# Second block: the selected and local scores of two heads issued in pairs, the compressed mask added once per bank

## The reference, cut to what matters

```
s_c = einsum(qq, kc);  p_c = masked_softmax(s_c, cmp_end <= t)      # compressed: 15 keys
...
s_s = einsum(qq, k_g); m_s = tok <= t                                # selected blocks
p_s = masked_softmax(s_s, m_s)
...
s_w = einsum(qq, kwb)                                                # local window of 512
p_w = masked_softmax(s_w, m_w)
return gg[0] * o_c + gg[1] * o_s + gg[2] * o_w
```

## Time and profile before

| | |
|---|---|
| median of 3 runs | 969.4 us (962.84 to 970.59) |
| profiled execution | 968.41 us |
| its span in the trace | 966.7 us |
| TensorE / VectorE / ScalarE / GpSimd busy | 93% / 71% / 53% / 33% |
| mean granted TensorE clock | 0.952 |

### The profile page before, as it was taken

How to read it: one execution, slowest core, us unless ns; L and a number is a source line. 1 busy time by engine, 2 the same in 40 slices (tenths; PEclk the granted TensorE clock), 3 DMA queues, 4 the chain that set the end, 5 groups by cost and what they waited for, 6 DMA issues and landing times.

```text
span 966.7 us, 16928 instructions
## 1 busy us (share of the span) xinstructions
PE 897.8 (93%) x6718; PEld 855.5 (88%) x6718; DVE 683.5 (71%) x986; ACT 511.3 (53%) x926; POOL 318.4 (33%) x150
## 2 busy tenths in 40 slices
PE   3997779999999998899999899999997999999998
PEld 3995669999999998787988789888996999999998
DVE  7857752899889994757889878844677476666573
ACT  5467445654565566765755654446344544444441
POOL 3644103122333323262655732222343223223220
PEclk8999789999999998999999999988898999999999
DMA  5834004354565654350755532221354456656641
GB/s 188 282 111 153 22 1 115 105 185 140 169 215 171 202 182 152 103 178 29 237 173 158 204 100 85 69 66 66 109 154 131 135 159 195 187 176 183 189 153 44
DMA packets 54078, 137.18 MB, mean 142 GB/s; under 512 B 6000, under 2 KB 24816, under 8 KB 53872
## 3 DMA queue, kind: packets, MB, share of 16 engines
q1 hardware_dynamic: 54000, 136.11, 44.5%
HBM read 135.03 MB, written 1.05 MB: 141 GB/s over the span
## 4 chain that ended last, share of the span: by engine, by line
PE 75%; DVE 16%; ACT 5%; issue 4%; DMA 0%; DVEq 0%; SPq 0%; ACTq 0%
PE PROD L578 14%; PE PROD L579 14%; PE PROD L580 14%; PE OP L763 3%; PE SC L719 3%; DVE wlo L1494 3%; DVE RS L1502 2%; PE PROD L640 2%; PE OP L578 2%; PE OP L580 2%; PE OP L579 2%; PE SC L578 2%; PE SC L579 2%; PE SC L580 2%; PE TP L580 2%
## 5 line engine op out<-in xcount | busy, mean ns | idle before, releaser
L561 POOL TENSOR_TENSOR wlo<-raw,whi 128x1024 fp32r<-128x1024 f32 x124 | 314.6, 2543 | 624.6 <-ACT whi L1014 624.5
L578 PE MATMUL PROD<-HA,whi 128*128 128x256 f32 x1096 | 320.4, 292 | 15.7 <-DVE HA L1522 8.8
L579 PE MATMUL PROD<-HA,wlo 128*128 128x256 f32 x1096 | 315.6, 288 | 0.0
L580 PE MATMUL PROD<-HA,whi 128*128 128x256 f32 x1096 | 315.3, 288 | 0.0
L1014 ACT ACTIVATE whi<-raw 128x1024 fp32r<-128x1024 f32 x252 | 261.6, 1050 | 46.5 <-PE PROD L580 22.6
L1494 DVE TENSOR_TENSOR wlo<-raw,whi 128x1024 fp32r<-128x1024 f32 x128 | 186.8, 1463 | 96.2 <-ACT whi L1014 96.0
L578 PEld LDWEIGHTS PROD<-HA,whi 128*128 128x128 f32 x1096 | 216.6, 198 | 18.8 <-DVE HA L1522 9.4
L579 PEld LDWEIGHTS PROD<-HA,wlo 128*128 128x128 f32 x1096 | 216.4, 197 | 0.6 <-issue 0.5
L580 PEld LDWEIGHTS PROD<-HA,whi 128*128 128x128 f32 x1096 | 215.9, 197 | 0.0
L1776 DVE SCALAR_TENSOR_TENSOR YC<-Y,CV,YC 128x255 f32<-128x255 f32 x88 | 66.9, 762 | 2.2 <-ACT YC L1208 0.7
L1502 DVE RECIPROCAL RS<-RTT 128x256 f32<-128x256 f32 (+2 forms) x18 | 42.8, 2379 | 20.7 <-ACT RTT L1033 20.7
(11 more groups left out here) (319 smaller groups left out, 1724.0 us busy)
## 6 DMA issues: line engine op xcount, KB each, us to landing
raw<-stream SPq DMA_DIRECT2D x208, 512.0 KB, 3.8
raw<-stream SPq DMA_DIRECT2D x136, 128.0 KB, 2.4
raw<-stream SPq DMA_DIRECT2D x8, 384.0 KB, 3.1
raw<-stream SPq DMA_DIRECT2D x8, 256.0 KB, 3.1
X<-xT SPq DMA_DIRECT2D x2, 512.0 KB, 4.7
E<-memT SPq DMA_DIRECT2D x1, 1024.0 KB, 5.9
out<-X SPq DMA_DIRECT2D x8, 128.0 KB, 2.0
PX<-pT SPq DMA_DIRECT2D x1, 256.0 KB, 3.9
```

Source lines behind the costliest of these rows:

```text
L561: nc.gpsimd.tensor_tensor(wlo[:, n % NSPLIT, :], raw[:, n % NRAW, :], whi[:, n % NSPLIT, :].bitcast(F32), ALU.subtract).then_inc(lo_pool, 1)
L578: nc.tensor.matmul(dst, wh, hi, start=start, stop=False, skip_group_check=True)
L579: nc.tensor.matmul(dst, wl, hi, start=False, stop=False, skip_group_check=True)
L580: last = nc.tensor.matmul(dst, wh, lo, start=False, stop=stop, skip_group_check=True)
```

## The change

In `scores`, the selected and local units issue the score matmuls of an even and an odd head one behind the other, and then the two masks. The compressed units issue the scores of all eight heads, and then one mask matmul for each bank that covers its four heads (60 columns, the mask read four times through a broadcast). There only the first head of each bank starts an accumulation. The `mem` and `mla` units stay as they were.

```diff
@@ -708,22 +708,32 @@
                     at = score_at(kind, j)
+                    first = True
...
                     elif kind == "cmp":
                         a, b = QN[half, h // 2, q], KCD[half, (h // 4) * CMP:(h // 4 + 1) * CMP]
+                        first = j < 2
...
-                    last = nc.tensor.matmul(SC[:, at:at + kw], a, b, start=True, stop=kind == "mem",
+                    last = nc.tensor.matmul(SC[:, at:at + kw], a, b, start=first, stop=kind == "mem",
                                             skip_group_check=True)
-                    if kind == "cmp":
-                        last = nc.tensor.matmul(SC[:, at:at + kw], identb[:, :], cmpb[:, qt, :], start=False,
-                                                stop=True, skip_group_check=True)
-                    elif kind != "mem":
+                    if kind == "mla":
                         last = nc.tensor.matmul(SC[:, at + kw - P:at + kw], identb[:, :], causalb[:, :], start=False,
                                                 stop=True, skip_group_check=True)
+                    elif kind in ("slc", "win") and j % 2:
+                        for i in (j - 1, j):
+                            at = score_at(kind, i)
+                            last = nc.tensor.matmul(SC[:, at + kw - P:at + kw], identb[:, :], causalb[:, :],
+                                                    start=False, stop=True, skip_group_check=True)
+                if kind == "cmp":
+                    for r in range(2):
+                        last = nc.tensor.matmul(
+                            SC[:, 512 * r:512 * r + 4 * CMP].rearrange("p (i k) -> p i k", k=CMP), identb[:, :],
+                            cmpb[:, qt, :].unsqueeze(1).to_broadcast((P, 4, CMP)), start=False, stop=True,
+                            skip_group_check=True)
                 last.then_inc(s_ready, 1)
```

## The result

The changed kernel takes 954.2 us (median of four, 951.5 to 956.1), the one before 968.8 in the same comparison (962.8 to 970.6): a ratio of 0.986, 95% interval 0.981 to 0.991. That is 14.6 us less, where 957.8 was forecast, so the direction, the size and the range (948.5 to 965) held. The trace says that the sum was not right in all its terms: the lengths and the waits that it names came out within a few tenths, two waits of about 1 us each were missing, and the clock term was several times too small. (A ratio leaves out disturbed executions, so it is not always the quotient of the medians.)

The account below looks back on a forecast made before the run. TensorE was taken as the bound, with 3.6 us idle in the stage. 13.9 us gross less waits of 0.4 and 3.4, plus 1.5 for the clock, gave 11.6 off 969.4: 957.8 us, range 948.5 to 965.

Parts of the forecast that it names:

- the clock term: Stage of the second block: one low-rate stretch of 3.4 us at 1.2 GHz fewer, 1.5 us gained.
- Overlap of the halves: Paired scores on two array halves: both heads cost about the time of one, the second 0.01 us.
- Rival 1: Score pairs: halves don't overlap, only switches and twelve masks go; 7.1 us gross, 5.8 net, 963.6 us; chance 0.13.
- Lengths, 13.9 us gross: Shorter second-block units: 5.5 us from 256-key pairs, 3.9 from 128-key pairs, 4.5 from both compressed units.
- The copy into PT at the compressed units: Values product behind compressed scores waits for ScalarE's copy: 0.1 and 0.3 us, 0.4 lost.
- VectorE's taps: Convolution taps from selected 0 on: VectorE only 5.1 us earlier, so TensorE waits 1.3 before turning selected 2.
- product behind selected 3's scores: Values product there waits for ScalarE's PT copy: 5.45 us earlier and not 8.8, 3.4 lost in all.
- From selected 3's values product on: Four local units behind it, where VectorE has slack: 1.0 + 1.0 + 1.4 + 1.4 = 4.8 us gained.
- Rival 3: Clock holds at 1.00 behind shorter stretches: up to 7.5 us on top of 10.1, about 951.5; chance 0.21.
- my 10.1 net: Whole stage without the clock: 13.9 us gross less waits of 0.4 and 3.4.
- Rival 2: Between selected 0 and 2, one more slow stretch of VectorE's taps takes 4.4 us: about 963; chance 0.15.
- Rival 4: Stage: saved time becomes TensorE idle time and the granted clock falls; slower than before, about 984 us; chance 0.04.

Follow-up runs that it names:

- no_overlap: The changed kernel with the heads of one half, their masks, then the other half, so no halves run side by side; 957.4 us, 0.987 of the kernel before.
- thrice: The changed kernel with every compressed, selected and local score pair issued three times, masks once behind the last; 960.7 us, 0.992 of the kernel before.
- score_twice: The kernel before with each score matmul of compressed, selected and local units issued twice in a row; 980.7 us, ratio 1.013.
- halves_in_turn: The changed kernel with one mask matmul per bank behind all four selected or local scores, even heads issued before odd, compressed too; 956.4 us, one execution.

## Why the prediction was right, and what it had too small

The number held in part by luck: the clock gave several times what I had for it, and the rest gave somewhat less.

- **Overlap of the halves (rows 6).** Right; two records start together in the selected scores, and no_overlap gives its price. Rival 1 is out.
- **Lengths, 13.9 us gross.** From first score to values product, the ten units took 28.1 us before (3.4 and 3.5; 2.3, 2.2, 3.1, 3.1; the same for the local ones). Now two pairs take 1.6 or 1.2 to 1.3 where nothing is waited for, the compressed scores 1.2 with their masks. Right within 0.1 us a unit.
- **The copy into PT at the compressed units, 0.4 us.** Right: the product starts at 575.66 behind a copy that ends at 575.61, and at 588.74 behind one that ends at 588.69, 0.28 idle.
- **VectorE's taps.** Right in place, and in size within 0.4 us. The timeline of VectorE after, against the earlier trace rows:

```profile
603.81 0.69 DVE L1985 TENSOR_TENSOR KMEM<-OP,rsum 128x512 f32<-128x512 f32 x1 [0.17 <-PE OP L773]
604.53 5.31 DVE L1920 SCALAR_TENSOR_TENSOR CY<-U,CV,CY 128x237 f32<-128x237 f32 x14
...
621.72 1.23 DVE L1568 TENSOR_REDUCE mx<-SC 128x4 f32<-128x1024 f32 x1
```

  From the first compressed score to this maximum it was 622.44 - 569.35 = 53.1 us and is 47.4, 5.7 earlier (about 5 forecast). The turn of selected 2 waits 0.94 (1.3 forecast), the product behind selected 3's scores 1.87 (2.05). Counted from the same point that product is 6.0 us earlier (5.45 forecast). Two waits were missed: TensorE waits 1.87 for VectorE before it turns the memory output (0.85 before), and 1.27 for the exponentials behind the scores of local 2. The timeline of TensorE at both (a fence for each):

```profile
579.59 0.66 PE L783 MATMUL TP<-ident,OMEM 128*128 128x128 f32 x4 [1.87 <-DVE OMEM L1588]
```

```profile
666.96 0.33 PE L749 MATMUL TP<-ident,PR 128*128 128x128 f32 x1 [1.27 <-ACT PR L1083]
```

- **The clock, 1.5 us: mis-sized.** The stage had 30.7 us at 1.2 GHz and has 10.2, six stretches of 3.4 fewer and not one. thrice, with units as long as before, prices it in the stage: 161.6 - 152.1 = 9.5 us, and the lengths with their waits are the other 6.1 of the 15.6. Those are single traces, and the whole executions split it otherwise. Of the 48 of the kernel before, 20 ran at a mean clock of 0.957 to 0.963 and took 964.6 us on average; the change at 0.957 and 0.959 took 954.8 and 956.1. That is about 9 us less at the same clock, which leaves 5 to 6 of the 14.6 to the clock. Both ways it is several times 1.5; between 5 and 9.5 the split is not settled. I had the cause wrong too: I took the length of the stretches of small matmuls for it, and thrice, with the old length, keeps the clock. From selected 3's values product on I had 4.8 us; it was 10.6: 4.8 of lengths, less 1.3 for the wait at local 2, and about 7 of clock (17 us fewer at 1.2 GHz, five stretches). Before that point the forecast wait for VectorE and ScalarE took what a faster TensorE gave.
- **Rival 3** (the clock holds) was nearest to what happened in the second half of the stage; the forecast's number held because my 10.1 net was more than the lengths brought, by 4 us in the traces and by 1 in the executions at the same clock, with TensorE waiting at two more places. Rival 2 did not come: the taps took 5.31 and 5.85 us, as in the trace of before (5.32 and 5.85). Its time by its own terms was 962.2 and not 963. Rival 4 is out: idle time grew by 6.9 us and the clock rose.

## What to carry to other kernels

Scores of heads on two halves of the array belong side by side, and full-array matmuls such as masks behind them: in this kernel a unit of 256 keys went from 3.05 to 1.61 us with the masks behind each pair, and to 1.30 with them behind all four heads, which no longer showed in the time. What hides behind the shortened work must be listed before the gain is added up; the lists of VectorE and ScalarE held TensorE for 2.8 us at selected 2 and 3, and moving one small item in ScalarE's list gave 1.6 of the stage back. Where a stage shows the lower clock level, price a change that packs TensorE's work closer by that too, and compare kernels of equal length, or executions at the same mean clock, to tell the clock from the work.

## What the runs showed that was not expected

- The time follows the clock from execution to execution: 48 executions of the kernel before took 962.7 us at a mean granted clock of 0.959 up to 982.3 at 0.933. That is more than the change brings, and one trace of each kernel does not settle 3 us. The traced execution of before had 0.952.
- Doubling the work of the local scores (score_twice) left the local segment 0.9 us shorter in its trace than in that of before: 13.7 us at 1.2 GHz were gone, and gave back more than the 5.2 us that the work cost. The time of the whole kernel was 13.9 us longer.
- The two halves of the array run matmuls out of program order: with the even heads issued first, scores of the odd half start together with them when two heads stand ahead, and 0.47 us late when four do (halves_in_turn, 1.30 us a unit in either order, but 1.53 against 1.07 for the compressed scores).
